# Six conditioning units added up by VectorE inside the first MLP, instead of four before the expert loop and two in the last attention

## The reference, cut to what matters

```
def ada_modulation(c, w, b):
    m = jax.nn.silu(c) @ w + b
    shift, scale, gate = jnp.split(m[:, None, :], 3, axis=-1)
    return shift, scale, 1.0 + gate
...
    for layer in range(DEPTH_2):
        shift, scale, gate = ada_modulation(c, ada_w[layer, 0], ada_b[layer, 0])
        h = x * (1.0 + scale) + shift
        y = mixer_ab(h, ...) if layer % 2 == 0 else mixer_c(h, ...)
        x = layer_norm(DN_ALPHA * x + gate * y, ln_g[layer, 0], ln_b[layer, 0])
        shift, scale, gate = ada_modulation(c, ada_w[layer, 1], ada_b[layer, 1])
        h = x * (1.0 + scale) + shift
        y = squared_relu_mlp(h, mlp_w1[layer], mlp_w2[layer])
        x = layer_norm(DN_ALPHA * x + gate * y, ln_g[layer, 1], ln_b[layer, 1])
```

## Time and profile before

| what | value |
|---|---|
| three runs | 1815.35, 1816.06 (median), 1817.51 us |
| the profiled execution, its own time | 1816.24 us |
| its span between first and last instruction | 1814.3 us |
| mean granted TensorE clock | 0.992 |
| busy: TensorE, VectorE, ScalarE, GpSimd | 1743.7, 749.0, 526.5, 26.6 us |
| read from memory | 585.5 MB |
| first expert's matmuls begin, loop's last end | 253.7 us, about 1173 us |
| first MLP begins and ends on TensorE | 1308.2 us, about 1487 us |

### The profile page before, as it was taken

How to read it: one execution, slowest core, us unless ns; L and a number is a source line. 1 busy time by engine, 2 the same in 40 slices (tenths; PEclk the granted TensorE clock), 3 DMA queues, 4 the chain that set the end, 5 groups by cost and what they waited for, 6 DMA issues and landing times.

```text
span 1814.3 us, 24405 instructions
## 1 busy us (share of the span) xinstructions
PE 1743.7 (96%) x9906; PEld 1092.5 (60%) x9906; DVE 749.0 (41%) x1287; ACT 526.5 (29%) x698; POOL 26.6 (1%) x36
## 2 busy tenths in 40 slices
PE   8999999999999999999999999999899999999997
PEld 7688754444434434343434344375699888679986
DVE  4454342212212112121212121379865469676555
ACT  5344421111111111111111010248444453744442
POOL 0002000000000000000000000000000000000001
PEclk9999999999999999999999999998999999999999
DMA  9958899999999999999999999974355556435550
GB/s 350 348 212 336 316 404 426 428 427 428 428 428 428 428 428 428 429 429 428 428 429 428 429 429 429 418 282 177 116 186 185 192 194 228 153 116 185 185 208 24
DMA packets 96608, 587.43 MB, mean 324 GB/s; under 512 B 7150, under 2 KB 7364, under 8 KB 70948
## 3 DMA queue, kind: packets, MB, share of 16 engines
q1 hardware_dynamic: 95072, 582.27, 79.3%
q10 hardware_dynamic: 1476, 4.30, 0.7%
HBM read 585.51 MB, written 1.05 MB: 323 GB/s over the span
## 4 chain that ended last, share of the span: by engine, by line
PE 72%; DMA 20%; DVE 5%; ACT 2%; issue 1%; SPq 0%; DVEq 0%; ACTq 0%
PE bank L1274 31%; DMA ring<-in_w_gate_up 19%; PE bank L1587 15%; PE bank L1606 9%; PE bank L1533 4%; PE bank L1861 3%; PE bank L1353 1%; PE bank L1617 1%; PE bank L1265 1%; PE bank L1579 1%; DVE w_lo L565 1%; ACT arena L965 1%; DMA ring<-in_ada_w 1%; PE bank L1599 1%; PE bank L1988 0%
## 5 line engine op out<-in xcount | busy, mean ns | idle before, releaser
L1587 PE MATMUL bank<-ring,arena 128*64 128x512 f32 x2048 | 462.4, 597 | 28.4 <-DMA ring<-in_w_gate_up 27.8
L1587 PEld LDWEIGHTS bank<-ring,arena 128*64 128x64 f32 x2048 | 137.7, 136 | 319.3 <-issue 255.9
L1606 PE MATMUL bank<-ring,arena 128*64 128x512 f32 x1024 | 226.8, 595 | 3.3
L1274 PE MATMUL bank<-w_hi,arena_r 128*128 128x512 f32 x672 | 217.1, 391 | 1.9 <-DVE arena_r L2705 1.9
L565 DVE TENSOR_TENSOR w_lo<-ring,w_hi 128x4096 fp32r<-128x4096 f32 (+2 forms) x44 | 192.5, 4375 | 44.1 <-ACT w_hi L554 41.8
L2400 DVE TENSOR_SCALAR arena<-bank 128x512 f32<-128x512 f32 x32 | 22.1, 691 | 367.2 <-PE bank L1587 367.2
L963 ACT ACTIVATE arena<-arena,sb_tab 128x512 f32<-128x512 f32 x32 | 23.1, 722 | 508.7 <-DVE arena L2400 508.7
L554 ACT ACTIVATE w_hi<-ring 128x4096 fp32r<-128x4096 f32 (+2 forms) x43 | 152.3, 3583 | 31.6 <-DMA ring<-in_c_w_out 18.3
L1606 PEld LDWEIGHTS bank<-ring,arena 128*64 128x64 f32 x1024 | 71.9, 137 | 137.6 <-issue 132.1
L1274 PE MATMUL bank<-XT_r,w_hi 128*128 128x256 f32 x512 | 145.8, 285 | 4.4 <-DVE arena_r L2689 4.4
L1274 PE MATMUL bank<-arena_r,w_hi 128*128 128x256 f32 x512 | 144.9, 283 | 0.0
(11 more groups left out here) (415 smaller groups left out, 2104.6 us busy)
## 6 DMA issues: line engine op xcount, KB each, us to landing
ring<-in_w_gate_up SPq DMA_DIRECT2D x128, 2048.0 KB, 32.0
ring<-in_w_down SPq DMA_DIRECT2D x64, 2048.0 KB, 35.3
ring<-in_mlp_w SPq DMA_DIRECT2D x32, 2048.0 KB, 8.3
ring<-in_ada_w SPq DMA_DIRECT2D x21, 2048.0 KB, 13.1
ring<-in_c_w_in SPq DMA_DIRECT2D x6, 2048.0 KB, 7.7
ring<-in_w_in SPq DMA_DIRECT2D x4, 2048.0 KB, 8.8
ring<-in_w_v SPq DMA_DIRECT2D x2, 2048.0 KB, 9.6
ring<-in_w_out SPq DMA_DIRECT2D x2, 2048.0 KB, 11.9
```

What stands on the lines that cost most here:

```text
L1274: mm = pe.matmul(out, st[a], mv[b], start=start and a + b == 0, stop=stop and a == 1, skip_group_check=True)
L1587: mm = pe.matmul(B[m][CAP * h:CAP * h + CAP, :], xe[:, 2 * j + kl, :], w[:, kl, m * D + h * HW:m * D + (h + 1) * HW], start=False, stop=(j ...
L1606: mm = pe.matmul(B[2][CAP * h:CAP * h + CAP, :], hT[:, c, CAP * j:CAP * j + CAP], w[:, c, h * HW:(h + 1) * HW], start=(j == 0 and c == 0), ...
```

## The change

Twelve units instead of 16 stand ahead of the loop: none in the projection, two behind it, three in the mixer, and one, three and three later as before. The first attention keeps six late units, now 12 to 17. The second attention has none. Units 18 to 23 go to the first MLP. SyncE cuts each into eight pieces of 128x512 (256 KB) and brings them into three places (`unit_raw`), each piece when the one three before it was consumed. VectorE multiplies the first piece by a scalar per partition and adds the product of each next one (`unit_rows`): four rows between the remainder of the half's second bank and the first `split_lo`, one between the two `split_lo`, three behind, in each half of iterations 0 to 2. TensorE sums the partitions of two units with eight matmuls of one column (`unit_sums`) behind the w1 granule of half p = 0 in iterations 1 to 3. The loops over the first MLP's groups are written out; `gate_rows(1)` moves into the last group's first half.

In SyncE's one queue the pieces stand between the weight fills: fills 0 to 3, unit 18, fills 4 and 5, unit 19, fills 6 and 7, and so on to fills 14 and 15.

```diff
-LATE = 16
-ADA_AT = [("k", 2), ("v", 3), ("mix", 4), ("q", 1), ("scores", 3), ("router", 3)]
-ADA_GROUPS = [(0, 2, 7, 6), (2, 5, 7, 6), (5, 9, 3, 2), (9, 13, 6, 7), (13, 16, 1, 4)]
+LATE = 12
+LAST = 18
+ADA_AT = [("k", 0), ("v", 2), ("mix", 3), ("q", 1), ("scores", 3), ("router", 3)]
+ADA_GROUPS = [(0, 2, 7, 6), (2, 5, 3, 2), (5, 9, 6, 7), (9, 12, 1, 4)]
...
-HEAD = [("w_k", 0), ("w_k", 1), ("ada", 0), ("w_v", 0), ("ada", 1), ("w_v", 1), ("ada", 2), ("ada", 4), ("w_in", 0), ("ada", 3)]
-TAIL = [("w_o", 0), ("w_o", 1), ("ada", 12), ("ada", 14), ("ada", 15), ("ada", 13)]
+HEAD = [("w_k", 0), ("w_k", 1)]
+TAIL = [("w_o", 0), ("w_o", 1), ("ada", 8), ("ada", 10), ("ada", 11), ("ada", 9)]
...
-        + [("c_in", i) for i in range(6)] + [("late", 3)] + [("c_out", i) for i in range(2)] + [("mlp1", i) for i in range(16)])
+        + [("c_in", i) for i in range(6)] + [("c_out", i) for i in range(2)] + [("mlp1", i) for i in range(16)])
...
+        unit_raw = [arn(a, HW) for a in (4096, 4608, 7312)]
+        def unit_acc(n):
+            return XN[:, 1, HW * (n % 2):HW * (n % 2) + HW]
...
+                def unit_fill(n):
+                    w = A["ada_w_2"][1, 1].rearrange("(k p) n -> p k n", p=P)
+                    for m in range(8 * n, 8 * n + 8):
+                        if m >= 3:
+                            sp.wait_ge(sem("unit_used"), m - 2)
+                        sp.dma_start(unit_raw[m % 3], w[:, m % 8, HW * n:HW * n + HW]).then_inc(
+                            sem(f"unit{m % 3}_landed"), 16)
+                if l == 0:
+                    for n in range(16):
+                        mlp_fill(n // 4, n % 4)
+                        if n % 2 and 3 <= n <= 13:
+                            unit_fill((n - 3) // 2)
...
-            project(MEMT, 0, between={2: first_units, 4: ada_combine, 6: mix_turn})
+            project(MEMT, 0, between={6: mix_turn})
             chunk_ready("mix", KC - 1)
-            ada(3)
+            pe.wait_ge(sem("cs"), 2)
+            ada(2)
...
-            ada(4)
+            ada(3)
...
-                    if st == "cc" and u == 6:
-                        pe.wait_ge(*upto("cc", "pte", 12))
-                        late_combine(LATE + 6, 5, 400)
-                        late_combine(LATE + 7, 5, 404)
...
+                    if l == 0 and p == 0 and it:
+                        unit_sums(it - 1)
...
+                    if l == 0 and last:
+                        pe.wait_ge(sem("late_read"), 3)
+                        gate_rows(1)
+            def unit_sums(i):
+                for n in (2 * i, 2 * i + 1):
+                    pe.wait_ge(sem("unit_used"), 8 * n + 8)
+                    for c in range(4):
+                        mm = pe.matmul(B[6][:, 4 * n + c:4 * n + c + 1], unit_acc(n)[:, c * P:(c + 1) * P], ones[:, 0:1],
+                                       start=True, stop=True)
+                    mm.then_inc(sem("late_comb"), 1)
...
-                    if st == "cc" and u == 0:
-                        late_copies()
...
+                    by_unit = l == 0 and not last
+                    if by_unit:
+                        unit_rows(2 * it + p, 0, 4)
                     if not (last and p == 1):
                         split_lo(dve, n, 2 * p + 2, it)
+                        if by_unit:
+                            unit_rows(2 * it + p, 4, 5)
                         split_lo(dve, n, 2 * p + 3, it)
+                        if by_unit:
+                            unit_rows(2 * it + p, 5, 8)
...
+            def unit_rows(n, a, b):
+                acc = unit_acc(n)
+                for k in range(a, b):
+                    m = 8 * n + k
+                    dve.wait_ge(sem(f"unit{m % 3}_landed"), 16 * (m // 3 + 1))
+                    if k == 0:
+                        if n >= 2:
+                            dve.wait_ge(sem("late_comb"), 6 + n - 1)
+                        ins = dve.tensor_scalar(acc, unit_raw[m % 3], sil[:, 1, 0:1], None, ALU.mult)
+                    else:
+                        dve.wait_ge(sem("unit_used"), m)
+                        ins = dve.scalar_tensor_tensor(acc, unit_raw[m % 3], sil[:, 1, k:k + 1], acc, ALU.mult, ALU.add)
+                    ins.then_inc(sem("unit_used"), 1)
```

More of the change, by code:

```diff
@@ L715, in _, with mlp_fill @@
                 w2 = A["mlp_w2_2"][l].rearrange("(k p) n -> p k n", p=P)
[L716 to L726, removed]
+                def mlp_fill(i, j):
+                    s = slot_of(g + j)
+                    sp.wait_ge(used, i * R2 + (g + j - R2 + 1))
+                    if j % 2 == 0:
+                        src = w1[:, :, bass.ds(i * (2 * HW) + (j // 2) * HW, HW)]
+                        dst = slot(s).rearrange("p (k n) -> p k n", k=8)
+                    else:
+                        src = w2[:, bass.ds(i * 8 + (j // 2) * 4, 4), :]
+                        dst = slot(s).rearrange("p (k n) -> p k n", k=4)
+                    sp.dma_start(dst, src).then_inc(landed[s], 16)
+                def unit_fill(n):
[10 more added lines that the diff above has]
+                            unit_fill((n - 3) // 2)
+                else:
+                    with sp.Fori(0, 4) as i:
+                        for j in range(R2):
+                            mlp_fill(i, j)
                 g += 16
@@ L951, in _ @@
             act.wait_ge(sem("bias_landed"), 16 * 8)
-            act.wait_ge(*done("ada", 13))
+            act.wait_ge(*done("ada", 9))
             for m in range(2):
@@ L1049, in mlp_group @@
                                        bias=zero).then_inc(sem("mlp_sq"), 1)
+                    if l == 0 and last and p == 0:
+                        act.wait_ge(sem("late_comb"), 12)
+                        act.activation(mod[:, 3, :], B[6][:, 0:24], ACT.Copy).then_inc(sem("late_read"), 1)
                     if not (last and p == 1):
@@ L1173, in _ @@
                 mlp_group(0, it, False)
-            gate_rows(1)
             load_ln(1, upto("ln0", "ln_x", 2))
@@ L1936, in mlp_group @@
                     mm.then_inc(used, 1)
-            def mlp(l):
-                with pe.Fori(0, 3) as it:
-                    mlp_group(l, it, False)
-                gate_rows(2 * l + 1)
-                mlp_group(l, 3, True)
+                    if l == 0 and last:
+                        pe.wait_ge(sem("late_read"), 3)
+                        gate_rows(1)
+            def unit_sums(i):
[5 more added lines that the diff above has]
+                    mm.then_inc(sem("late_comb"), 1)
+            def mlp(l):
+                if l == 0:
+                    for it in range(4):
+                        mlp_group(0, it, it == 3)
+                else:
+                    with pe.Fori(0, 3) as it:
+                        mlp_group(l, it, False)
+                    gate_rows(2 * l + 1)
+                    mlp_group(l, 3, True)
                 at[0] += 16
@@ L2561, in front @@
                                       ALU.subtract).then_inc(sem("nm"), 1)
-            def late_copies():
-                for u, b in ((LATE + 6, 6), (LATE + 7, 7)):
-                    if u == LATE + 6:
-                        dve.wait_ge(sem("late_mm"), 4)
-                    else:
-                        dve.wait_ge(*done("late", 3))
-                    for i, part in enumerate(late_part(u)):
-                        dve.tensor_copy(part, B[b][:, i * S:(i + 1) * S]).then_inc(sem("late_part"), 1)
             def attend(st, mask, ot, after_front):
@@ L2719, in mlp @@
                 affine(f"ln{2 * l}", range(TB))
-                with dve.Fori(1, 3) as it:
-                    mlp_group(l, it, False)
+                if l == 0:
+                    for it in (1, 2):
+                        mlp_group(0, it, False)
+                else:
+                    with dve.Fori(1, 3) as it:
+                        mlp_group(l, it, False)
                 mlp_group(l, 3, True, ahead)
```

114 lines of the change are left out of this document (51 added, 63 removed).

## The result

After the change the kernel takes 1821.12 us (median of seven runs, 1817.22 to 1821.42) where before takes 1815.24 on the same chip: ratio 1.0029, 95% interval 1.0017 to 1.0041. Run again beside later experiments it came out at 1.0030 (1.0021 to 1.0039). So it is slower, by 5.3 us by that ratio (the medians are 5.9 apart), where 2.5 less was forecast. The profiled execution took 1820.36 us, its span 1818.5 (before 1814.3).

The account below looks back on a forecast made before the run. Bound: TensorE, busy 1743.7 of 1814.3 us, up to 593 us, then the expert loop's unbroken weight stream. Sum: 1816.2 - 9.8 - 2.5 + 4.8 + 5.0 = 1813.7 us; range 1808.5 to 1819.0.

Parts of the forecast that it names:

- Ahead of the loop, -9.8: Before the expert loop: fewer units win 9.3 us around the projection and 0.5 in the mixer, 9.8 us in all.
- Rival D: Expert loop: its stream is held by something not moved, so 9.8 us are lost again; 1823.5 us, chance 0.05.
- Second attention, -2.5: Second attention: without its units, VectorE's copies and TensorE's combining go; 2.5 us won, between 1 and 3.5.
- `unit_sums`, +4.8: First MLP: three times eight one-column matmuls on TensorE's path, 1.6 us each time, 4.8 us added.
- Waits in the MLP, +5.0: First MLP: TensorE waits for late splits in six halves of iterations 0 to 2, 5.0 us in sum.
- last of its six terms: First MLP, iteration 2, second half: TensorE's wait forecast at 1.5 us.
- the second: First MLP, iteration 0, second half: pieces queue behind 4 MB of weight fills; TensorE's wait 1.3 us.
- the first: First MLP, iteration 0, first half: fourth row ends 6.8 us after T, a w1 granule's end; TensorE waits 0.4 us.
- The third and fourth: First MLP, iteration 1: waits of 0.35 us behind late rows and `affine` (first half) and 1.5 us (second half).
- A: The forecast itself: the MLP gives back 8.7 to 15.9 of 12.3 us won; likeliest 1813.7 us, chance 0.45.
- B: First MLP: pieces overtake or fills leave earlier, stall per half under 0.4 us; 1809.7 us, chance 0.38.
- C: First MLP: waits drop TensorE's clock to half, six dips of 1.8 us add 10.6; 1824.3 us, chance 0.10.

Follow-up runs that it names:

- e2_none: Kernel after without units 18 to 23 (no pieces, rows or unit sums), last conditioning vector filled from other data; 1801.83 us, ratio to before 0.9931.
- e9_after: Kernel after itself run once more, nothing changed; ratio to before 1.0030.
- e4_ln: Kernel after with ScalarE's two layer norm loads issued behind `gate_rows(1)` in the last group's first half; 1815.02 us, ratio to before 1.0003.
- e5_order: Kernel after with three rows ahead of the first `split_lo`, two between; three pieces ahead of the w1 fill, five between w1 and w2 fills; 1808.99 us.
- e7_order_only: Kernel after with only SyncE's order changed: three pieces ahead of the w1 fill, five between w1 and w2 fills; 1838.34 us.
- e1_rows: Kernel after with three rows ahead of the first `split_lo` and two between, instead of four and one; 1817.65 us.

## Why the prediction was wrong

The time predicted was 1813.7, the range up to 1819.0; 1821.12 came. The steps, with the profile's 1820.36 against 1813.7 (6.7 us):

- **Ahead of the loop, -9.8.** In the pair of profiles -8.6. Over twelve profiles with the same program up to there the MLP starts at 1298.3 on average, 9.9 before that of before. But before has one profile, and its execution (1816.24) lies 1.0 to 2.4 us above before's medians (1815.24, 1813.89, 1814.37), so as much of the 9.9 may be its scatter. In the projection the steps are as told: TensorE waits 0.82 us for w_v's remainder (0.8 forecast), and both units run at full clock. The projection won 10.5 - 0.9 = 9.6 (predicted 9.3). In the mixer the last unit's transfer was the limit (8.07 us in the chain, the estimate was 8); from 68.40 to the unit's end, 128.57, it is 60.2 us where it was 139.8 - 78.9 = 60.9: 0.7 won for 0.5. The wait of about 1 us for VectorE that was to follow did not come; TensorE waited 0.79 for the transfer instead. The size is right, and in the mixer in part by luck.
- **Through the loop.** The first expert's matmuls start 11.1 us earlier, the last scatter ends 9.6 earlier. Rival D is out.
- **Second attention, -2.5.** -3.3. By e2_none both gains are 12.5 us, for 12.3 predicted.
- **`unit_sums`, +4.8.** 5.04. Right.
- **Waits in the MLP, +5.0.** Here the forecast failed, in the last of its six terms (0.4, 1.3, 0.35, 1.5, 0 and 1.5). That last "1.5", for iteration 2, second half, measured 4.11, and 1.3 more in half clock behind it. It used a landing time of 3.1 us read where nothing else moved (89 GB/s at 43 us, about this transfer alone), and did not ask what another queue issues in that stretch. `load_ln(1)` was in the kernel before, held back by `gate_rows(1)`; the edit that moved `gate_rows(1)` let it out among the pieces. In the stage account: 14.4 = 9.8 + 2.6 (the last interval, 26.8 for 24.2) + 1.3 (clock) + 0.7, which is left open.
- **The other five terms.** The working behind the second is right: the first piece was expected 15.2 us behind the start of the w1 granule and was consumed at 15.5; the wait was to be 1.3 and is 1.26. For the first, 0.4 was forecast and 0.4 was in hand: the fourth piece landed after 2.5 us, and its row ended at T + 6.0 instead of T + 6.8. The third and fourth measured nothing in after, where 1.8 us of half clock at 1359 had made TensorE late by itself, and 0.64 and 2.08 in e9_after, without that fall. So the sum of waits, 5.4 for 5.0, agrees by luck. What did come true is the length that the circle gives: in e4_ln the whole MLP takes 182.78, where 172.76 + 9.8 = 182.6 was predicted, though with 2.3 us of waits and 1.8 of half clock.
- **The formula beside the row.** The formula that the prediction takes from the Trainium skill ("DMA: Bandwidth & Descriptors", section Anatomy of one DMA) is fitted there to transfers that GpSimd issues. SyncE issues these, and their median is 3.2 us, not 2.6.
- **Clock elsewhere.** 1.7 us of the difference is a fall at the start of the second MLP, 0.79 in the window at 1624 us. Of the other profiles some have it (e5_order: 193.7 us from there to the end) and some do not (192.4 in e9_after), whatever the kernel. It belongs to the scatter and not to the change.
- **Rivals.** A named the mechanism, its bounds (8.7 to 15.9 given back in the MLP) hold the 14.4, but with 1.7 from the clock elsewhere and 1.2 less ahead the sum left its range. B is refuted: pieces do queue behind fills (e7_order_only). C was right in kind and too large: one fall behind a wait cost 1.3 us, and there was one such in after and two in e9_after, not six.

The ratio (+5.3 us) agrees with the stages (+4.2) within its interval. By its ratio, 1.0003 (0.9994 to 1.0012), e4_ln is still slower than the 0.14% gain that was forecast, and its MLP is as forecast; where the rest lies no pair of profiles shows.

## What to carry to other kernels

Where one engine's order and one queue's order wait for each other, follow the whole circle and compare its period with the engine that it must keep up with. One link shortened alone (e1_rows) or reordered alone (e7_order_only) wins little or loses much; cut in the right place (e5_order), it made even slow transfers free.

In these runs a small transfer with a tight round trip was priced by what had been issued just ahead of it, on its own queue (e7_order_only) and on another (e4_ln). List the other engines' loads in the stretch before taking a quiet moment's landing time. And where an edit moves a wait, ask what stood behind it: moving `gate_rows(1)` set two loads free 9 us earlier, and the longest wait of the first MLP came of it.

## What the runs showed of the hardware

A piece of 256 KB landed 3.2 us after its issue in the median (after), and 5.0 beside 1 MB issued on another queue in the us before.

TensorE waited for `split_lo` 20 times in seven profiles. Behind the 13 waits of 0.3 to 1.7 us the next granule's clock stayed at 1.00. Behind all seven of 2.1 us and more (after, e9_after, e7_order_only) it fell: the windows of 4 us behind e7_order_only's waits of 3.51, 3.42, 3.44 and 6.21 us show 0.62, 0.64, 0.57 and 0.50, those behind its waits of 1.57 and 1.55 us show 1.00. Falls without such a wait just ahead were seen too, behind the sums and at the start of the second MLP.

The MLP's start shows a scatter of 4 us between identical programs, as large as the effects in question; the stage alone repeated to 0.01 us where TensorE never waited for `split_lo` (178.04, 178.05, 178.05, 178.05) and scattered by 1.4 where it did (187.17, 188.56).
